# Weight tiles read with a step of two elements: column tiles of a pair interleaved in the chunk

## The reference

```python
def swiglu(h, w_gate, w_up, w_down):          # w_gate, w_up: 1024 x 2816, w_down: 2816 x 1024
    return (jax.nn.silu(h @ w_gate) * (h @ w_up)) @ w_down

h = h + 0.5 * swiglu(rms_norm(h, g), w_gate, w_up, w_down)   # four of these
...
# two MLPs 1024 -> 4096 -> 1024 (squared ReLU), and per mixer an input and an output projection
```

## Time and profile before

| | |
|---|---|
| median of 3 runs | 1692.23 us (1691.09 to 1692.69) |
| the profiled execution | 1690.46 us, of which the span of its instructions is 1688.7 us |
| TensorE matmul (PE) busy | 1603.4 us, 95% of the span, 13068 matmuls |
| TensorE weight load (PEld) busy | 1534.2 us, 91% |
| VectorE (DVE), ScalarE (ACT), GpSimd (POOL) busy | 64%, 45%, 28% |
| mean granted TensorE clock | 0.969 of full |
| one chunk's DMA, issue to landing | 4.9 us (median) |

### The profile page before, as it was taken

One profiled execution on the slowest core, in us unless ns is written; L12 is line 12 of the kernel. 1 busy time (PEld: TensorE's weight loads), 2 busy tenths in 40 slices (PEclk: granted clock), 3 DMA queues, 4 the chain that ended last, 5 costly groups with the idle time before them and its releaser, 6 DMA issues.

```text
span 1688.7 us, 31471 instructions
## 1 busy us (share of the span) xinstructions
PE 1603.4 (95%) x13068; PEld 1534.2 (91%) x13068; DVE 1081.2 (64%) x1067; ACT 761.1 (45%) x995; POOL 470.2 (28%) x413
## 2 busy tenths in 40 slices
PE   5989998799999999999899999999999997999997
PEld 5989997699999999999789999976999996699997
DVE  7698769866555665564566555635655665476555
ACT  5424350154434543447554343655444355654432
POOL 6999627610000100016530000564100023510000
PEclk9999996799999999999999999989999997999999
DMA  6535540055555555554435555450555552045552
GB/s 220 211 124 199 199 151 1 1 175 175 178 198 189 172 199 199 180 192 149 152 102 178 199 188 196 140 184 1 175 197 179 196 174 76 25 168 199 181 198 75
DMA packets 39012, 265.74 MB, mean 157 GB/s; under 512 B 4352, under 2 KB 6400, under 8 KB 7328
## 3 DMA queue, kind: packets, MB, share of 16 engines
q1 hardware_dynamic: 37808, 261.41, 45.0%
q0 software_dynamic: 1136, 3.38, 0.8%
HBM read 263.70 MB, written 1.06 MB: 157 GB/s over the span
## 4 chain that ended last, share of the span: by engine, by line
PE 78%; DVE 10%; POOL 7%; issue 2%; ACT 2%; DMA 0%; DVEq 0%; SPq 0%; POOLq 0%; ACTq 0%
PE ps L539 72%; POOL tsq L284 2%; PE ps L829 2%; PE ps L819 2%; DVE gst L1455 2%; DVE wlo L1275 2%; DVE xlo L1281 1%; PE ps L807 1%; POOL trr L377 1%; DVE h L1291 1%; DVE tk L1505 1%; PE ps L714 1%; POOL tsq L285 1%; DMA h<-in_xT 0%; POOL pm L403 0%
## 5 line engine op out<-in xcount | busy, mean ns | idle before, releaser
L1275 DVE TENSOR_TENSOR wlo<-raw,whi 128x2048 fp32r<-128x2048 f32 x246 | 596.3, 2429 | 247.4 <-ACT whi L969 247.0
L539 PE MATMUL ps<-xhi,whi 128*128 128x256 f32 x2048 | 574.5, 280 | 26.2 <-DVE wlo L1275 13.4
L969 ACT CAST whi<-raw 128x2048 fp32r<-128x2048 f32 x246 | 469.4, 1912 | 252.7 <-PE ps L539 252.7
L539 PE MATMUL ps<-xlo,whi 128*128 128x256 f32 x2048 | 571.3, 279 | 0.0
L539 PE MATMUL ps<-xhi,wlo 128*128 128x256 f32 x2048 | 570.8, 279 | 0.0
L539 PEld LDWEIGHTS ps<-xhi,whi 128*128 128x128 f32 x2048 | 389.2, 190 | 30.7 <-DVE wlo L1275 14.4
L539 PEld LDWEIGHTS ps<-xhi,wlo 128*128 128x128 f32 x2048 | 389.5, 190 | 0.0
L539 PEld LDWEIGHTS ps<-xlo,whi 128*128 128x128 f32 x2048 | 388.7, 190 | 0.1
L539 PE MATMUL ps<-hhi,whi 128*128 128x256 f32 x1216 | 341.8, 281 | 0.2
L539 PE MATMUL ps<-hhi,wlo 128*128 128x256 f32 x1216 | 341.6, 281 | 0.0
L539 PE MATMUL ps<-hlo,whi 128*128 128x256 f32 x1216 | 341.3, 281 | 0.0
(11 more groups left out here) (235 smaller groups left out, 2074.1 us busy)
## 6 DMA issues: line engine op xcount, KB each, us to landing
raw<-in_wstream SPq DMA_DIRECT2D x247, 1024.0 KB, 4.9
h<-in_xT SPq DMA_DIRECT2D x1, 1024.0 KB, 8.3
out_hT<-h SPq DMA_DIRECT2D x2, 512.0 KB, 3.0
biasA<-bias_rows POOLq DMA_DIRECT2D x5, 192.0 KB, 5.2
biasB<-bias_rows POOLq DMA_DIRECT2D x3, 192.0 KB, 5.4
braw<-in_s5b POOLq DMA_DIRECT2D x1, 512.0 KB, 3.9
CL<-in_s5c POOLq DMA_DIRECT2D x4, 128.0 KB, 5.0
tg<-in_tgain POOLq DMA_DIRECT2D x1, 384.0 KB, 3.5
```

The costliest lines, as they stand in the source:

```text
L539: return pe.matmul(o, l, r, start=first, stop=last, skip_group_check=True)
L969: act.copy(whi[:, slot, :], raw[:, slot, :]).then_inc(S("whi_ready"), 1)
L1275: dve.tensor_tensor(wlo[:, slot, :], raw[:, slot, :], whi[:, slot, :], ALU.subtract)\
```

## The change

The host stores the two column tiles of each pair interleaved: element 0 of tile 0, element 0 of tile 1, element 1 of tile 0, and so on. A column tile of 128 elements is then read with a step of two elements, over 1024 bytes of a partition in place of 512. The chunks whose weights are stationary operands are stored so; the token-major chunks and that of `keys` are not. The kernel's instructions are the same in number, order, operands' sizes and waits; only the stationary operands' access patterns in `proj`, `proj_first` and `down` differ.

```diff
-        whi_d = [whi[:, s, :].rearrange("p (f m) -> p f m", f=2) for s in range(NSLOT)]
-        wlo_d = [wlo[:, s, :].rearrange("p (f m) -> p f m", f=2) for s in range(NSLOT)]
+        def feature_tile(w, slot, k, m):
+            return w[:, slot, :].rearrange("p (k c m) -> p k c m", k=KT, m=2)[:, k, :, m]
+
+        def row_tile(w, slot, f, dt):
+            return w[:, slot, :].rearrange("p (f d c e) -> p f d c e", f=2, d=KT // 2, e=2)[:, f, dt // 2, :, dt % 2]
...
             # proj and proj_first
-                        w = slice(m * P, (m + 1) * P)
-                        last = mm3(half_bank(bank, m), whi_b[slot][:, k, w], wlo_b[slot][:, k, w],
+                        last = mm3(half_bank(bank, m), feature_tile(whi, slot, k, m), feature_tile(wlo, slot, k, m),
                                    ohi[:, k, :], olo[:, k, :], k == 0, k == KT - 1)
...
             # down
-                        w = slice(dt * P, (dt + 1) * P)
-                        last = mm3(half_bank(dt // 2, dt % 2), whi_d[slot][:, f, w], wlo_d[slot][:, f, w],
+                        last = mm3(half_bank(dt // 2, dt % 2), row_tile(whi, slot, f, dt), row_tile(wlo, slot, f, dt),
                                    hid_hi(b)[:, f, :], hid_lo(b)[:, f, :], False, final and f == 1)
...
+def stationary(chunks):
+    n, p, c = chunks.shape
+    return chunks.reshape(n, p, c // (2 * P), 2, P).transpose(0, 1, 2, 4, 3).reshape(n, p, c)
...
 def by_rows(w):
     f, d = w.shape
-    return w.reshape(f // (2 * P), 2, P, d).transpose(0, 2, 1, 3).reshape(f // (2 * P), P, 2 * d)
+    return stationary(w.reshape(f // (2 * P), 2, P, d).transpose(0, 2, 1, 3).reshape(f // (2 * P), P, 2 * d))
+
+def by_column_tiles(w):
+    return stationary(by_feature(w, 2 * P))
```

More of the change, by code:

```diff
@@ L1669, in swiglu @@
     def swiglu(l, s):
-        return interleaved([by_feature(a["ffn_w_gate"][l, s], 256), by_feature(a["ffn_w_up"][l, s], 256)],
+        return interleaved([by_column_tiles(a["ffn_w_gate"][l, s]), by_column_tiles(a["ffn_w_up"][l, s])],
                            by_rows(a["ffn_w_down"][l, s]))
     def mlp(l):
-        return interleaved([by_feature(a["mlp_w1_2"][l], 256)], by_rows(a["mlp_w2_2"][l]))
+        return interleaved([by_column_tiles(a["mlp_w1_2"][l])], by_rows(a["mlp_w2_2"][l]))
     down = np.zeros((D, 512), np.float32)
@@ L1680 @@
         swiglu(0, 0),
-        by_feature(a["s5_w_in"][0], 256), by_feature(a["s5_w_glu"][0], 256), by_feature(a["s5_w_out"][0], 256),
+        by_column_tiles(a["s5_w_in"][0]), by_column_tiles(a["s5_w_glu"][0]), by_column_tiles(a["s5_w_out"][0]),
         swiglu(0, 1), swiglu(1, 0),
-        by_feature(a["moba_w_qkv"][0], 256), by_feature(a["moba_w_out"][0], 256),
+        by_feature(a["moba_w_qkv"][0], 256), by_column_tiles(a["moba_w_out"][0]),
         swiglu(1, 1),
-        by_feature(a["ab_w_in_2"][0], 256)[list(AB_ORDER)], by_feature(a["ab_w_out_2"][0], 256),
+        by_feature(a["ab_w_in_2"][0], 256)[list(AB_ORDER)], by_column_tiles(a["ab_w_out_2"][0]),
         mlp(0),
-        by_feature(down, 256), widened(by_feature(a["c_w_uq_2"][0], 768)), ukv, by_feature(a["c_w_out_2"][0], 256),
+        by_feature(down, 256), widened(by_feature(a["c_w_uq_2"][0], 768)), ukv, by_column_tiles(a["c_w_out_2"][0]),
         mlp(1)])
```

## The result

The changed kernel takes 1732.88 us (median of 4 runs, 1728.15 to 1742.49) against 1691.66 us (median of 4 runs of the kernel before beside it): ratio 1.0254, 95% interval 1.0233 to 1.0275. It is 41 us slower where 49 us less were forecast; the time lies inside the stated range, in the part that the range had been stretched to for rival A.

The account below looks back on a forecast made before the run. PE's matmul pitch was taken to bound the kernel: savings of 16.6 + 25.5 + 6.7 = 48.8 us give 1690.5 - 48.8 = 1641.7 us profiled, plus 1.8 for the median, say 1643 us. Range 1620 to 1742.

Parts of the forecast that it names:

- rival A: Weight loads beside streams: twice the stationary requests bring more collisions; pitch up to 120.7 ns, 1737 to 1743 us; chance 0.22.
- the span in the steady stretches is count times pitch: SwiGLU and MLP stages: PE never rests, so a changed matmul pitch changes the span one for one.
- DVE and ACT keep their times: Chunk pipeline: casts and subtractions write the same 2048 packed elements, 1912 and 2429 ns; those edits cost nothing.
- at half clock: Matmuls at half clock: pitch must stay 213.3 ns; the few there gain nothing.
- load and stream are about equally long: Matmuls at full clock: load and stream both last about the pitch, read SBUF together and delay each other a little.
- equal rates, less loss: Changed matmuls: both operands walking 1024 bytes in the same time lose less; 48.8 us saved, likeliest case; chance 0.58.
- all kinds at 111.3 ns: Input-side (proj), down and output-projection matmuls: middle estimate of the new pitch, saving 16.6 + 25.5 + 6.7 = 48.8 us.
- The floor: Matmul with a 128-column load: lowest pitch 109.3 ns, from sixteen packed transposes; all kinds reaching it would save 70 us.
- The price of the load by itself: Stationary loads at a step of two: the load keeps its rate, so the step by itself costs 0 us.
- The forecast's row: Sixteen S5 matmuls, moving operand at step two: 1.82 us, no longer than packed 1.91; taken as speaking against a doubled load.
- B: Stationary loads: step two halves the load's rate, adding 97.6 x 10,560 = 1031 us, about 2720 us; chance 0.08, whole or part.
- C: Matmul pitch: the two reads don't disturb each other, so the step changes nothing, 1692 us; chance 0.12.

Follow-up runs that it names:

- experiment 1: Bare probe of the proj pattern, not the reference: widths and load steps varied; 256 columns took 113.3, 120.0, 235.6 ns at steps 1, 2, 4.
- experiments 3 and 7: 3: step two in down alone, 1.0093, or all but down, 1.0187, against the kernel before. 7: bare probe, distances and entries varied, 113.3 or 117.8 ns at 192.
- experiments 5 to 7: Bare probes varying load step, stream width (5, 6), distance and entry (7); 128 columns took 111.5 to 111.7 ns packed, 117.8 to 120.0 at step two.
- experiment 6: Bare probe with load steps 1 to 8, then a moving operand of step two: 116.7 ns at 128 columns, 229 at 256; packed 112 and 113.
- experiment 2: Bare probe, 256 columns, 12 distances between moving and stationary tile: 113.3 to 120.0 ns packed; at step two 120.0, at one distance 120.9.
- experiment 4: Tiles moved to distance 0 modulo 256: the packed kernel before took 1730.58 us (1.0222), the changed kernel 1727.68 us (1.0218), both ratios to the kernel before.

## Why the prediction was wrong

**What held.** That the span in the steady stretches is count times pitch: the rise of the pitches gives 42.2 us, the medians 41.2. That DVE and ACT keep their times and that no other wait takes over (PE's idle time went from 85.3 to 82.3 us). That at half clock nothing is lost (213.3 ns at step 2 in experiment 1). That load and stream are about equally long and that the timing between them matters (the earlier trace rows against each other; experiments 3 and 7).

**The step that failed** is "I take this as the likelier reading: equal rates, less loss". The forecast put all kinds at 111.3 ns; they came to 120.0. Equal walking speed of the two operands brings nothing: step 2 gave 120.0 ns at eleven distances, 120.9 at one and 120.7 at another. Packed it brings nothing either: 128 moving columns beside a load of 128 walk as fast as the load and took 111.7 ns, no less than 160 or 192 columns (experiments 5 to 7). The reading rested on one row, the plain float32 transposes at 109.3, which differ from the products in more than the rates. The floor taken from them was wrong too: with a narrow stream a packed load of the product kind takes 111.7 ns at every distance tried.

**The price of the load by itself** was put at nothing, and this is where the loss comes from. The forecast's row for it, sixteen matmuls with a moving operand of step two in 1.82 us, mixed matmuls that ran side by side: three of the sixteen start within 6 ns of another, and the others, after the first, follow each other at 113 to 114 ns, more than the packed 109.3. Read by its starts, the row gave no sign of a load at full rate. In the probe, on all 128 rows, such a moving operand takes 116.7 ns (experiment 6), 5 ns more than packed. The Trainium skill's rule in "SBUF — State Buffer" (under the DMA port swizzle: full rate with at least two hits on each 16-byte line) was cited as giving 0 us. The runs agree with it on the 16-byte line as the unit. They do not agree that two hits are enough: with exactly two a load takes 117.8 to 120.0 ns and not 111.7.

**The rivals.** A named the right sign and nearly the size: 1737 to 1743 us against 1732.9. Its mechanism is half right. That the step asks for twice as many pieces is what counts, but the loss does not grow with the stream: at 384 columns 3.8 ns, at 512 nothing. A's 120.7 ns was taken from the loss of a packed matmul of 384 columns, so its nearness to 120.0 is luck. B, the load slower by itself, is right in kind and was priced far too high, at a doubled load (97.6 ns a matmul, which should read 97.4); a doubled load is what step 4 does. C is out: the time moved by 2.5%. The Trainium skill's rule cited for it ("SBUF — State Buffer", who interferes with whom), two independent read ports and a PE that never waits, does not hold between PE's own two reads: the pitch of packed matmuls changes from 113.3 to 120.0 with the distance between the two operands' addresses alone (experiment 2). These runs did not test it between engines.

**What the loss is made of.** A pitch of 113.3 ns is out of reach for a load that takes 117.8 by itself. Of the 6.7 ns between 113.3 and 120.0 that accounts for 4.5; the other 2.2 appear with a stream of 256 columns beside it, at nearly all places alike, and are not explained. A bad distance alone takes a packed load to the same 120.0, and the two don't add up (experiment 4), so a kind that had a bad distance already lost little or nothing. Only proj on xhi/xlo was at the good distance, so it pays 35.6 of the 42 us; down was already at 118.3 and the output projections at 120.0.

**Open.** Why the distance works modulo 256 bytes, what decides which of the two rhythms a stream enters, and where the 3.8 ns at 384 columns come from, was not found. The exact 120.0 ns (9/8 of 106.7) that both a poor distance and the step of two end at is measured and not explained.

## What to carry to other kernels

When loads and streams on TensorE are equally long, read the pitch and not the busy share, and for each pair of operands by itself: two tiles' places in SBUF, shifted by some tens of bytes, were worth 4 ns on each of 3648 matmuls, 5 on 768 more, and 0.8% of the kernel. Keep the stationary operand packed; a step of two already makes its load the longer part, a step of four doubles the time. A row that stands in for an operation that the trace doesn't have should differ from it in one thing only; if it doesn't, a probe kernel of a few hundred matmuls settles in one run what rows can't.

## What the runs showed of the hardware

- A 128-column float32r load costs 111.7 ns packed at full clock (with 32 to 192 moving columns), and at steps of 2, 3 and 4 about 1.82 ns for each 16-byte piece touched (117.8 to 120, 174, 234 ns). At half clock a load costs 213.3 ns at steps 1 to 3; at step 4 it is 233.3 ns at either clock.
- Packed matmuls of 256 columns with a load each take 113.3 to 120.0 ns by the distance of the two operands modulo 256: 113.3 or 117.8 at 192 and 64, 117.3 at 160, 117.8 at 32, 118.3 at 224, 118.7 at 128, 120.0 at 0 and 96.
- These two rhythms at 192 and 64 come with the same instructions and addresses, and each lasts: a stretch of some 170 us stayed in the worse one.
- 384 and 512 packed moving columns take 173.3 and 233.3 ns, 13 and 20 above their 160 and 213.3 ns of streaming, also where the load is hidden.
